# Three weight loads, each sent as a transfer of 120 partitions and a transfer of eight

## Chip, cores and metric

One Trainium2 chip, one of its cores. The metric is the device time of one execution in microseconds (us), lower is better. The kernel before was run three times: median 1458.31 us, 1456.86 to 1459.31. The profiler also recorded one execution, and all durations below come from that one.

## What is computed

The reference is a stack of transformer-like blocks on 256 tokens of width 1024, all in float32. The change lies in the expert layer of the first block:

```python
def one(xc):                                   # a chunk of 128 tokens
    q = (xc @ w_q).reshape(C, 8, 2, 128)       # 8 heads of queries, w_q is 1024 x 2048
    s = einsum('chpd,hpnd->chpn', q, subkeys)  # scores against 128 keys, twice a head
    sv, si = lax.top_k(s, 16)
    ...                                        # the 16 best of the 16 x 16 pairs: ids, g
    ue = jnp.take(u, ids, axis=0)              # rows of 1024 from a table of 16384
    ve = jnp.take(v, ids, axis=0)
    a = gelu(einsum('cd,chkd->chk', xc, ue))
    return einsum('chk,chkd->cd', g * a, ve)
```

Before it stands a mixer of differential and grouped-query attention, behind it stand two layers with a Fourier mixer, windowed attention and a gated feed-forward part.

## The kernel before, in words

The expert layer runs as 16 stages: 8 heads times 2 chunks of 128 tokens, with head h in stages 2h and 2h + 1. A stage has 16 gathers. One gather (L819, issued by GpSimd's queue) fetches, for each of the 128 tokens, one row of 2048 floats (the rows of `u` and `v` side by side, 8192 bytes), so it fills 128 partitions with 8192 bytes each: 1 MB. There are 256 gathers in all. They go into 13 places, some in the weight ring (`ring`), some in the scratch area (`arena`). A place is reused when the matmuls that read it are done (`pair_free`). For each gather VectorE makes the dot product with the token (L2273), ScalarE the GELU and a diagonal matrix of the weights (L1745, L1749), and TensorE adds the weighted rows with two matmuls (L1223).

Between the stages TensorE makes the queries of the next head (L1196) from that head's slice of `w_q`: 128 partitions by 8192 bytes, 1 MB. The slice of head 0 lies in the tile `wqb`, those of heads 1 to 4 are loaded ahead into tiles of their own. The slices of heads 5, 6 and 7 go into `wqb` too, one after the other, while the gathers run: these are the three loads of the change. SyncE's queue (SP) issues each (L783) once the matmuls that read the slice before it are done (`q_done`), and TensorE waits for it (L1192) before it makes the queries of that head. The semaphore `wq_in` counts 16 for each transfer.

Behind the third load SP waits for the last gather but one (L785) and for free ring places (L787), and then loads the weights of the first layer that follows (L789, L790, L752). SP has nothing else to issue during the gathers.

Of the kernel before, what the change touches and what calls it, by code (L numbers as in the profile page):

```python
# [21 lines left out]
KD = D // P  # L22
# [33 lines left out]
def in_end(b):  # L56

    return sum(IN_PIECES[:b + 1])
# [16 lines left out]
def slot_end(j):  # L75

    return max(p for p, (i, q) in enumerate(PIECE_AT) if i <= j) + 1
# [11 lines left out]
KEPT = 4  # L89
# [27 lines left out]
def place(n, k):  # L117
    return ORDER[TOPK * n + k]


def turn_of(n, k):
    return TURN[TOPK * n + k]
# [34 lines left out]
UNIT_HEADS = ((0, 4, 1, 5, 2, 6, 3, 7), (4, 5, 6, 7, 0, 1, 2, 3))  # L157
OUT_ORDER = (4, 5, 6, 7, 0, 1, 2, 3)
QPAIRS = ((0, 1), (2, 3), (4, 5), (6,), (7,))

class Chain:

# [19 lines left out]
def program(nc, x, ctx, const, lpar, b1w, wq, sk, uv, lw, out):  # L182
    with ExitStack() as stack:
# [3 lines left out]
        def sem(name):  # L187
            return stack.enter_context(nc.semaphore(name))
# [47 lines left out]
        def small(*shape):  # L236
# [126 lines left out]
        const_in, const2_in, x_in, ctx_in, lpar_in, sk_in, wq_in = (sem(n) for n in (  # L363
            "const_in", "const2_in", "x_in", "ctx_in", "lpar_in", "sk_in", "wq_in"))
# [57 lines left out]
        def lslot(j):  # L422
            return ring[:, (B1_SLOTS + j) % RING, :]
# [14 lines left out]
        def transposes(pe, g0, tiles, off=0, base=0):  # L438

            for i, blocks in enumerate(tiles):  # L440
                g = g0 + i
                tile_free(pe, g, off)
                for j, b in enumerate(blocks):
                    last = nc.tensor.transpose(ps[:, base + g % TB, j * P:(j + 1) * P], b, ident)
                last.then_inc(tile_done, 1)
# [100 lines left out]
        def ops_qk():  # L546
            return ([[(kT[:, k, :], 0, 512, None, None)] for k in range(5)]
                    + [[(qT[:, k, :], i * S, i * S + S, None, None) for i, k in enumerate(pair)] for pair in QPAIRS])

# [176 lines left out]
        @block.sync  # L726
        def _(sp):
            head = CO["lam"][0]
            sp.dma_start(cst[:, 0:head], const[:, 0:head]).then_inc(const_in, 16)
            def b1_used(n):  # L730

                if n < MOD_A:
                    sp.wait_ge(a_raw, n + 1)
                    sp.wait_ge(a_lo, 2 * (n + 1))
                elif n in IN_SLOT:
                    sp.wait_ge(in_lo, in_end(IN_SLOT.index(n)))
                else:
                    sp.wait_ge(mod_sum, KD * (MODB_SLOT.index(n) + 1))

            def l_used(l, j):  # L740

                if j == 3:
                    sp.wait_ge(yt_done, l * 2 + 2)
                elif j == 4:
                    sp.wait_ge(l_yf, l * 2 + 2)
                else:
                    sp.wait_ge(w_lo, l * PL + slot_end(j))

            def load_layer(l, j):
                n = B1_SLOTS + j  # L750
                w = SLOT_WIDTH.get(j, SLOT)
                sp.dma_start(ring[:, n % RING, 0:w], lw[l, j, :, 0:w]).then_inc(slot_in[n % RING], 16)  # L752


            for n in range(B1_SLOTS):
                if n >= RING:
                    b1_used(n - RING)
                w = 2048 if n == IN_SLOT[1] else SLOT
                at = SLOT // 2 if n < MOD_A else 0
                if at:  # L760
                    sp.dma_start(ring[:, n, 0:at], b1w[n, :, 0:at]).then_inc(half_in[n], 16)
                sp.dma_start(ring[:, n % RING, at:w], b1w[n, :, at:w]).then_inc(slot_in[n % RING], 16)
                if n == 1:
                    sp.dma_start(ctxr, ctx.rearrange("(c p) d -> p c d", p=P)).then_inc(ctx_in, 16)
                    sp.dma_start(xr[:, :, :], x.rearrange("(c p) d -> p c d", p=P)).then_inc(x_in, 16)
                if n == MOD_A + 1:
                    sp.dma_start(cst[:, head:CW], const[:, head:CW]).then_inc(const2_in, 16)
                    sp.dma_start(g1b, const[:, CW:CW + D]).then_inc(g1_in, 16)
            sp.dma_start(lps[:, :, :], lpar.rearrange("l p n -> p l n")).then_inc(lpar_in, 16)
            sp.wait_ge(modcol_done, MOD_A + MOD_B)  # L770
            sp.dma_start(wqb[:, :, :], wq[0, :, :].rearrange("p (k n) -> p k n", k=KD)).then_inc(wq_in, 16)
            sp.wait_ge(in_used, IP)
            sp.dma_start(skb[:, :], sk).then_inc(sk_in, 16)
            last = KEPT - 1
            sp.dma_start(wq_kept[:, :, :], wq[KEPT, :, :].rearrange("p (k n) -> p k n", k=KD)).then_inc(kept_in[last], 16)
            sp.wait_ge(sc_done, 16)
            for i in range(last):
                if i == 2:
                    sp.wait_ge(pt_done, 16)
                sp.dma_start(kept_wq[i], wq[i + 1, :, :].rearrange("p (k n) -> p k n", k=KD)).then_inc(kept_in[i], 16)  # L780
            for h in range(KEPT + 1, PH):
                sp.wait_ge(q_done, 1 if h == KEPT + 1 else h)
                sp.dma_start(wqb[:, :, :], wq[h, :, :].rearrange("p (k n) -> p k n", k=KD)).then_inc(wq_in, 16)  # L783

            sp.wait_ge(pair_in[place(STAGES - 1, TOPK - 2)], 16 * turn_of(STAGES - 1, TOPK - 2))  # L785
            for j in range(RING):
                sp.wait_ge(pair_free, NS + max(LAST_USE[2 * j], LAST_USE[2 * j + 1]))  # L787
                if j == 0:
                    sp.dma_start(lslot(0)[:, 0:2 * PIECE], lw[0, 0, :, 0:2 * PIECE]).then_inc(first_in, 16)  # L789
                    sp.dma_start(lslot(0)[:, 2 * PIECE:SLOT], lw[0, 0, :, 2 * PIECE:SLOT])\  # L790
                        .then_inc(slot_in[B1_SLOTS % RING], 16)
                else:
                    load_layer(0, j)
            for l in range(LAYERS):
                for j in range(RING, LSLOTS):
                    l_used(l, j - RING)
                    load_layer(l, j)
                for j in range(RING if l + 1 < LAYERS else 0):
                    l_used(l, LSLOTS - RING + j)
                    load_layer(l + 1, j)  # L800
            for i in range(4):
                c, part = i % 2, slice((i // 2) * 512, (i // 2 + 1) * 512)
                sp.wait_ge(dn_out, 4 * LAYERS - 3 + i)
                sp.dma_start(out[c * P:(c + 1) * P, part], xr[:, c, part]).then_inc(out_done, 16)
            sp.wait_ge(out_done, 64)
# [50 lines left out]
        def _(pe):  # L856
# [112 lines left out]
            for p, (b, q) in enumerate(IN_AT):  # L969
# [11 lines left out]
                if b == 4 and q == 1:  # L981
# [6 lines left out]
            transposes(pe, T_QK, [[krow[:, j, k * P:(k + 1) * P] for j in range(4)] for k in range(5)]  # L988
                       + [[qrow[:, j, k * P:(k + 1) * P] for k in pair for j in range(NC)] for pair in QPAIRS], base=TURN_BANK)
            pe.wait_ge(tile_act, T_BASE // 2)  # L990
# [196 lines left out]
            def all_queries(h):  # L1187

                if h <= KEPT:
                    pe.wait_ge(kept_in[h - 1], 16)  # L1190
                else:
                    pe.wait_ge(wq_in, 16 * (h - KEPT + 1))  # L1192
                head = kept_wq[h - 1] if h <= KEPT else wqb
                for s in range(2):
                    for k in range(KD):
                        last = nc.tensor.matmul(ps[:, 0, s * S:(s + 1) * S], head[:, k, s * P:(s + 1) * P], hT[:, k, :],  # L1196
                                                start=(k == 0), stop=(k == KD - 1))
                last.then_inc(q_done, 1)
# [14 lines left out]
            def keys(h):  # L1213

                all_queries(h)
                all_key_sums(h)
# [13 lines left out]
            back_to_rows(1, (0, 2))  # L1230
            pe.wait_ge(row_out, 4)
            all_queries(1)
            experts(0, 0, places=range(GROUP, 2 * GROUP))
            all_key_sums(1)
# [32 lines left out]
            for l in range(LAYERS):  # L1267
# [244 lines left out]
                for ft in range(FT):  # L1512
                    for t in range(2):
                        if ft >= 2:
                            pe.wait_ge(up_sum, l * 2 * FT + 2 * (ft - 2) + t + 1)
                        p = P_UP + 2 * ft + t
# [1192 lines left out]
```

## Time and profile before

| | |
|---|---|
| median of three runs | 1458.31 us |
| the profiled execution: its own time, its span | 1457.39 us, 1455.2 us |
| mean granted clock of TensorE | 0.965 |
| TensorE, VectorE, ScalarE, GpSimd busy | 90%, 76%, 44%, 21% |
| HBM read | 414.20 MB |
| gathers, all 256 | 36864 packets, 268.45 MB |
| transfers issued by SP | 13488 packets, 146.82 MB |

The span is the time from the first to the last instruction, and 2.2 us of the execution lie outside of it. Shares of busy time are means over stages with different limits: what a change in one stage is worth is read in that stage. "DMA share" is the mean busy share of the core's 16 DMA engines; it can stand a little over 1 because a packet's record overlaps the next one's.

### The profile page before, as it was taken

The numbers are of one execution on the slowest core, as the hardware profiler recorded it, in microseconds if no ns is written. First come the engines' busy times: TensorE is split into PE (matmuls) and PEld (weight loads), VectorE is DVE, ScalarE is ACT, GpSimd is POOL, SyncE is SP. The second block draws the span as 40 slices with busy tenths as digits, with TensorE's granted clock in tenths as the row PEclk, the third lists the DMA queues.
The fourth block names the chain that finished last, engine by engine and source line by source line (L and its number), as shares of the span: only waits on it lengthen the run. The fifth ranks groups of instructions, "written<-read, shape, count | busy, mean of one in ns | idle before, by whom it ended". The sixth has DMA issues, their size and how long they took to land.

```text
span 1455.2 us, 16512 instructions
## 1 busy us (share of the span) xinstructions
PE 1312.6 (90%) x5504; PEld 875.3 (60%) x5504; DVE 1109.0 (76%) x2316; ACT 633.1 (44%) x1322; POOL 310.5 (21%) x308
## 2 busy tenths in 40 slices
PE   9998898898797979698797799999999999999998
PEld 3876655453343424253343346678888887888887
DVE  6688857866776777766677777879998588799974
ACT  5343743312221222222222226567776455677752
POOL 0000004344444334344444430001111000011100
PEclk9999999999898989899898899999999999999999
DMA  9624468999999999999999997434544444345530
GB/s 391 275 116 184 164 255 330 420 421 422 408 421 422 421 421 421 422 421 421 419 416 408 419 422 281 166 125 147 201 175 176 154 140 169 116 180 194 206 145 29
DMA packets 50436, 416.31 MB, mean 286 GB/s; under 512 B 5552, under 2 KB 5680, under 8 KB 7088
## 3 DMA queue, kind: packets, MB, share of 16 engines
q0 software_dynamic: 36864, 268.45, 44.6%
q1 hardware_dynamic: 13488, 146.82, 26.4%
q8 instruction: 43, 0.70, 0.2%
q14 instruction: 41, 0.34, 0.1%
HBM read 414.20 MB, written 1.05 MB: 285 GB/s over the span
## 4 chain that ended last, share of the span: by engine, by line
PE 55%; DVE 20%; DMA 15%; issue 5%; ACT 3%; POOL 2%; DVEq 0%; SPq 0%; POOLq 0%; ACTq 0%
PE ps L1523 11%; PE ps L1223 9%; DMA ring<-in_uv,ids 8%; PE ps L1525 6%; DMA arena<-in_uv,ids 5%; PE ps L1313 4%; PE ps L1302 4%; PE ps L1310 4%; DVE ring L2273 3%; PE ps L1045 2%; DVE arena L2273 2%; PE ps L934 2%; PE ps L935 2%; PE ps L936 2%; PE ps L1196 1%
## 5 line engine op out<-in xcount | busy, mean ns | idle before, releaser
L1223 PE MATMUL ps<-ring,arena 128*128 128x512 f32 x632 | 293.9, 615 | 52.7 <-ACT arena L1749 52.6
L2273 DVE CUSTOM_DVE_ANT_0 ring<-ring,arena 128x1024 f32<-128x1024 f32 x158 | 190.4, 1224 | 86.3 <-DMA ring<-in_uv,ids 85.8
L1223 PEld LDWEIGHTS ps<-ring,arena 128*128 128x128 f32 x632 | 122.5, 197 | 214.4 <-issue 150.5
L1523 PE MATMUL ps<-hpair,arena_r 128*128 128x512 f32 x704 | 246.7, 395 | 0.0
L1223 PE MATMUL ps<-arena 128*128 128x512 f32 x392 | 188.7, 626 | 50.2 <-ACT arena L1749 50.2
L617 DVE TENSOR_TENSOR arena_r<-ring,arena_r 128x1024 fp32r<-128x1024 f32 x152 | 185.5, 1223 | 57.0 <-ACT arena_r L602 53.5
L819 POOL DMA_INDIRECT ring<-in_uv,ids x158 | 166.8, 1056 | 227.0 <-PE ps L1223 165.9
L1525 PE MATMUL ps<-hpair,arena_r 128*128 128x256 f32 x704 | 197.4, 280 | 0.0
L602 ACT ACTIVATE arena_r<-ring 128x1024 fp32r<-128x1024 f32 x152 | 159.1, 1054 | 58.0 <-PE ps L1313 53.9
L819 POOL DMA_INDIRECT arena<-in_uv,ids x98 | 106.7, 1089 | 358.6 <-issue 242.9
L1223 PEld LDWEIGHTS ps<-arena 128*128 128x128 f32 x392 | 77.1, 200 | 153.2 <-issue 91.9
L2273 DVE CUSTOM_DVE_ANT_0 arena<-arena 128x1024 f32<-128x1024 f32 x98 | 118.6, 1224 | 50.9 <-DMA arena<-in_uv,ids 50.6
L1523 PEld LDWEIGHTS ps<-hpair,arena_r 128*128 128x128 f32 x704 | 132.0, 187 | 30.9
L1749 ACT ACTIVATE arena<-cst,wts 128x128 f32<-128x128 f32 x256 | 87.9, 393 | 135.2 <-DVE wts L2266 82.6
L851 POOL TENSOR_TENSOR arena<-arena 128x256 f32<-128x256 f32 x44 | 36.1, 821 | 500.8 <-ACT arena L1891 500.8
L1525 PEld LDWEIGHTS ps<-hpair,arena_r 128*128 128x128 f32 x704 | 133.0, 189 | 0.0
L1745 ACT ACTIVATE gel<-dots 128x4 f32<-128x4 f32 (+2 forms) x68 | 13.9, 205 | 229.0 <-DVE dots L2273 229.0
L1302 PE MATMUL ps<-arena_r 128*128 128x512 f32 x240 | 67.3, 394 | 1.0 <-DVE arena_r L672 1.0
L1910 ACT ACTIVATE arena<-arena,lps 128x256 f32<-128x256 f32 x88 | 52.9, 602 | 32.7 <-DVE arena L2548 32.2
L1313 PE MATMUL ps<-arena_r 128*128 128x512 f32 x240 | 66.2, 390 | 0.0
L1310 PE MATMUL ps<-arena_r 128*128 128x512 f32 x240 | 66.2, 389 | 0.0
L2556 DVE SCALAR_TENSOR_TENSOR arena<-arena,lps 128x255 f32<-128x255 f32 x88 | 62.3, 708 | 0.0
(337 smaller groups left out, 1993.7 us busy)
## 6 DMA issues: line engine op xcount, KB each, us to landing
ring<-in_lw SPq DMA_DIRECT2D x39, 2048.0 KB, 7.8
ring<-in_b1w SPq DMA_DIRECT2D x14, 2048.0 KB, 8.8
ring<-in_b1w SPq DMA_DIRECT2D x9, 1024.0 KB, 16.8
ring<-in_lw SPq DMA_DIRECT2D x8, 1024.0 KB, 5.2
wqb<-in_wq SPq DMA_DIRECT2D x4, 1024.0 KB, 9.0
arena<-in_wq SPq DMA_DIRECT2D x3, 1024.0 KB, 13.4
ring<-in_uv,ids POOLq DMA_INDIRECT x158, 16.5
ring<-in_lw SPq DMA_DIRECT2D x2, 1088.0 KB, 9.9
```

The source lines that it names most:

```text
L602: nc.scalar.activation(high_of(l, p), piece_raw(p), ACT.Copy).then_inc(w_hi, 1)
L617: nc.vector.tensor_tensor(low_of(l, p), piece_raw(p), high_of(l, p).bitcast(F32), ALU.subtract)\
L819: pool.indirect_dma_start(pairs_at[at], None, uv, bass.IndirectOffsetOnAxis(ap=ids[:, c, k:k + 1], axis=0))\
L1223: last = nc.tensor.matmul(ps[:, 4 + 2 * c + b, :], diag[:, k % 4, :], vrows[place(n, k)][:, b * 512:(b + 1) * 512], start=(n == c and k == 0),
L1302: nc.tensor.matmul(dst, ah, high_of(l, p)[:, cols_], start=first, stop=False, skip_group_check=True)
L1310: last = nc.tensor.matmul(dst, al, high_of(l, p)[:, cols_], start=False, stop=end and rows_last, skip_group_check=True)
L1313: last = nc.tensor.matmul(dst, ah, low_of(l, p)[:, cols_], start=False, stop=end and not rows_last, skip_group_check=True)
L1523: nc.tensor.matmul(ps[:, bank, :].rearrange("p (t n) -> p t n", t=2), high_of(l, p)[:, cols_], hpair[:, :, k, :], start=(k == 0), stop=Fal ...
L1525: last = nc.tensor.matmul(ps[:, bank, S:2 * S], low_of(l, p)[:, cols_], hH[:, k, :], start=False, stop=(k == KD - 1), skip_group_check=True)
L1749: nc.scalar.activation(diag[:, k % 4, :], ident, ACT.Copy, scale=wts[:, c, k:k + 1])\
L2273: V.tensor_tensor_reduce(out=urows[at], in0=urows[at], in1=hrow[:, c, :], scale=1.0, scalar=0.0, op0=ALU.mult, op1=ALU.add, accum_out=dots ...
L2556: run(V.scalar_tensor_tensor(cx[:, 1:S], hx[:, 0:S - 1], cv[:, ft, 4 * t:4 * t + 1], cx[:, 1:S], ALU.mult, ALU.add))
```

## The change

Each of the three loads of `wqb` is issued as two transfers, first partitions 0 to 119, then partitions 120 to 127. The count that TensorE waits for is raised to match. The bytes, their source and their destination stay the same.

```diff
+WQ_ROWS = (slice(0, 120), slice(120, 128))
...
             for h in range(KEPT + 1, PH):
                 sp.wait_ge(q_done, 1 if h == KEPT + 1 else h)
-                sp.dma_start(wqb[:, :, :], wq[h, :, :].rearrange("p (k n) -> p k n", k=KD)).then_inc(wq_in, 16)
+                for rows in WQ_ROWS:
+                    sp.dma_start(wqb[rows, :, :], wq[h, rows, :].rearrange("p (k n) -> p k n", k=KD)).then_inc(wq_in, 16)
...
                 if h <= KEPT:
                     pe.wait_ge(kept_in[h - 1], 16)
                 else:
-                    pe.wait_ge(wq_in, 16 * (h - KEPT + 1))
+                    pe.wait_ge(wq_in, 16 + 16 * len(WQ_ROWS) * (h - KEPT))
```

## Rows read from the trace of the kernel before

**Rows 1.** The page, part 2: the span in 40 slices, the DMA lines.
```profile
DMA  9624468999999999999999997434544444345530
GB/s 391 275 116 184 164 255 330 420 421 422 408 421 422 421 421 421 422 421 421 419 416 408 419 422 281 166 125 147 201 175 176 154 140 169 116 180 194 206 145 29
```

**Rows 2.** Busy time by stretch, the whole of the saturated gathers.
```profile
core 0: us, PE busy (x) PEld busy (x) DVE busy (x) ACT busy (x) POOL busy (x), PEclk, DMA share, GB/s
243.00:850.00 607.00, 501.18 (x1257) 239.01 (x1256) 434.12 (x1085) 144.75 (x371) 258.94 (x242) 0.92 1.01 419
```

**Rows 3.** Waits of VectorE, 243 to 850 us: total us, times, longest.
```profile
DVE ring L2273 <- DMA ring<-in_uv,ids: 81.9, 66, 3.4
DVE arena L2273 <- DMA arena<-in_uv,ids: 47.5, 43, 1.3
```

**Rows 4.** The chain that ended last, 840 to 900 us: start, us, what.
```profile
857.58 20.47 DMA ring<-in_uv,ids
878.07 5.02 DMA ring<-in_lw
883.09 0.02 issue
883.11 1.06 ACT arena_r L602
884.17 0.02 issue
884.20 1.23 DVE arena_r L617
```

**Rows 5.** Busy time by stretch at the end of the gathers (columns as in rows 2).
```profile
870.00:873.00 3.00, 3.00 (x9) 1.32 (x8) 2.77 (x9) 0.20 (x1) 0.00 (x0) 1.00 1.03 423
...
874.00:875.00 1.00, 1.00 (x3) 0.38 (x2) 0.62 (x3) 0.28 (x2) 0.00 (x0) 1.00 0.55 229
875.00:876.00 1.00, 1.00 (x4) 0.51 (x3) 0.37 (x1) 0.33 (x1) 0.00 (x0) 1.00 0.16 66
...
877.00:878.00 1.00, 1.00 (x3) 0.38 (x2) 0.22 (x1) 0.50 (x2) 0.00 (x0) 1.00 0.06 25
```

**Rows 6.** DMA view, 876.25 to 878.75 us, in 40 slices.
```profile
GB/s 0 131 0 0 0 0 131 0 0 0 0 131 0 0 0 0 131 0 0 0 0 131 0 0 0 0 131 0 0 0 0 131 0 0 0 0 131 0 0 0
DMA packets 9, 0.07 MB, mean 26 GB/s; under 512 B 1, under 2 KB 1, under 8 KB 1
```

**Rows 7.** VectorE's last dot products, in order of time.
```profile
875.63 1.23 DVE L2273 CUSTOM_DVE_ANT_0 ring<-ring,arena 128x1024 f32<-128x1024 f32 x1 [0.74 <-DMA ring<-in_uv,ids]
...
878.07 1.23 DVE L2273 CUSTOM_DVE_ANT_0 ring<-ring,arena 128x1024 f32<-128x1024 f32 x1 [0.72 <-DMA ring<-in_uv,ids]
...
880.54 1.23 DVE L2273 CUSTOM_DVE_ANT_0 arena<-arena 128x1024 f32<-128x1024 f32 x1 [0.75 <-DMA arena<-in_uv,ids]
```

**Rows 8.** DMA view, 240 to 870 us: queues (packets, MB, share), issues.
```profile
q0 software_dynamic: 35791, 260.64, 99.8%
q1 hardware_dynamic: 432, 3.15, 1.2%
q8 instruction: 10, 0.16, 0.1%
q14 instruction: 18, 0.15, 0.1%
...
wqb<-in_wq SPq DMA_DIRECT2D x3, 1024.0 KB, 9.1
```

**Rows 9.** SP's second and third load of `wqb`, in order of time.
```profile
569.35 0.33 SPq L783 DMA_DIRECT2D wqb<-in_wq  x1
...
652.06 0.33 SPq L783 DMA_DIRECT2D wqb<-in_wq  x1
```

**Rows 10.** TensorE's use of the second and third load.
```profile
644.96 7.07 PE L1196 MATMUL ps<-hT,wqb 128*128 128x256 f32 x32
...
728.82 7.07 PE L1196 MATMUL ps<-hT,wqb 128*128 128x256 f32 x32
```

## The prediction

> **What bounds the kernel now.** I read the page's lines of slices first. The DMA engines are near full only in one stretch, slices 7 to 23, at about 421 GB/s [rows 1]; elsewhere TensorE carries the time. The stretch 243 to 850 us in one row shows a DMA share of 1.01, and TensorE 501, VectorE 434 and GpSimd 259 us busy of 607 [rows 2]. So the gathers are bound by DMA, not by an engine. VectorE's waits say the same: 81.9 + 47.5 = 129.4 us for gathers to land [rows 3]. 421 GB/s over 16 engines is 26.3 GB/s each, so a packet of 8192 bytes takes 0.311 us and eight of them 2.49 us. The 268.45 MB of 256 gathers are 128 rows of 8192 bytes each, eight rows to an engine if they are spread evenly.
>
> Then the end of the stretch, since a DMA-bound stretch is worth what it moves its last landing. The chain goes gather (landed 878.07), first layer weights (883.09), ScalarE, VectorE [rows 4]; the load at 878.07 stands behind SP's wait for the last gather but one. The reader should now look at the DMA share there: 1.03 to 873, 0.55 in 874 to 875, 0.16 in the next us and 0.06 in 877 to 878 [rows 5]. One engine of 16 is 0.0625. In 876.25 to 878.75 nine packets move, one each 0.31 us, at 26 GB/s [rows 6]: one engine is still at it alone, at full speed, with eight rows and one small packet, a whole gather's share. VectorE gets the last gathers at 875.63, 878.07 and 880.54, 2.45 us apart [rows 7], which is that engine's pace for eight rows. A gather is landed when its slowest engine is done, so **one engine sets every landing at the end**. The fifteen others were done with the last gather by about 876.2 (the share falls from 0.16 to 0.06 there, [rows 5]), the lagging one at 880.5 [rows 7]: a lag of 4.3 us. All sixteen were busy until 873, so what the last engine carries beyond the mean is paid in full.
>
> Why does it lag? Two queues of instruction fetches run beside the data: ten packets of 0.16 MB and eighteen of 0.15 MB in 240 to 870 us [rows 8]. At 26.3 GB/s they are 6.1 and 5.7 us of one engine. If the first queue is fixed to one engine and the second is spread, that engine would lag by 6.1 us less what the others get of the second: the size of the 4.3 us seen. This is my inference; no row names the engine of a packet.
>
> **The change, part by part.** A load of `wqb` is 128 rows of 8192 bytes: eight rows for each of 16 engines, 3 x 1 MB in all, 3.15 MB [rows 8].
>
> *The first part, 120 rows.* 120 is 15 x 8. Filled in eights, it leaves one engine without a row. That engine saves 8 x 0.311 = 2.49 us in each load, 7.5 us over three. The others keep their eight rows.
>
> *The second part, eight rows.* It goes to eight engines with one row each: +0.31 us on each of them a load, 0.93 us over three. The bytes stay the same; the sum over all engines is 0.
>
> *What lies on the path.* Only the last landing counts. If the engine left out is the lagging one, it would finish 7.5 us of work earlier, but the gain is capped by the next: the others' end, 4.3 us earlier. If the slowest of those is one of the eight with extra rows, it ends 0.93 us later than now, which leaves 3.4. Eight of sixteen have the rows and the share falls off over about 2 us [rows 5], so several engines are near each other and I take a value between, nearer the low end: 3.6 us. Bounds 3.0 and 4.3. The gain then goes through whole: VectorE waits 0.72 to 0.75 us for each of the last gathers [rows 7], the weights are issued when the last but one lands [rows 4], and with the share below 1 there is room for them. TensorE has 501 of 607 us of work in the stretch [rows 2], so it can follow.
>
> *The issues.* Each load costs SP one more instruction of 0.33 us [rows 9], 1 us in all. SP's queue has nothing else to issue until the gathers end; hidden. Without that cover it would be 1 us.
>
> *The wait of TensorE.* The load issued at 569.35 lands 9.1 us later [rows 8, 9] and is used at 644.96, the one of 652.06 at 728.82 [rows 10]: margins of 66 us. A second transfer behind the first adds at most its own row and a landing, far less. The count that TensorE waits for is that of both transfers; no engine waits longer. Cost 0; it would cost only if a load took over 66 us more.
>
> The Trainium skill ("DMA: Bandwidth & Descriptors", section "Why a DMA increments its semaphore by 16 and not by 1") says that a transfer runs on the largest number of engines up to 16 that divides its rows, taken from the lowest-numbered ones: 15 for 120 rows, which leaves out the last engine, and 8 for eight. The same page ("Latency and other measured facts") says that engines 7 and 15 are usually slower than the others in traces. Were the lagging engine 15, the sum would be the gain above; were it 7, a loss of 0.93 us. One engine does lag here, by 4.3 us, but no row gives its number.
>
> A rule of that page ("Rules for kernel authors") speaks against the change: splitting a transfer by partitions is not worth it, since the parts share the same engines. By it the sum would be 0. It tells nothing of a part that leaves an engine out.
>
> **The rivals.**
>
> *Forecast: the engine left out is the lagging one.* Speaks for it: exactly one engine lags [rows 5, 6], and an extra queue would be put at one end of the row of engines rather than in the middle, while rows dealt out in order leave the last one free. That is a judgement, not a row. 1457.4 - 3.6 = 1453.8 in the profiled execution. Chance 0.46.
>
> *Rival 1: the lagging engine is among the eight that take an extra row.* It then ends 3 x 0.31 = 0.93 us later and the engine relieved was never late: 1458.3 profiled. For it: eight of sixteen places, and the other end of the row is one of them. Chance 0.27.
>
> *Rival 2: it is among the seven that neither lose nor gain, or the split leaves no engine out* (the rows are spread over all sixteen some other way, so the change does not do what it says). No difference: 1457.4. Against the first half: it would lie in the middle. Chance 0.20.
>
> *Rival 3, the slower side: rows written by another engine than in a gather collide.* In the gathers, engine and partitions go together all the time. With 15 or 8 engines the partitions fall to others, and two engines may write into one group of partitions at once. If each of the 3 x 8 rows costs the lagging engine another packet's time, that is 24 x 0.311 = 7.5 us: 1464.9. It decides (over 2.9 us) from 0.12 us a row. No row shows a collision, as every large transfer here has 128 rows; against it, the loads are 1.2% of the engines' time [rows 8], and any collision with an engine that leads costs nothing up to 4.3 us. Chance 0.07.
>
> **How the numbers follow.** The profiled execution took 1457.39 us, 0.9 below the median of the runs, 1458.31. So the forecast is 1458.3 - 3.6 = 1454.7; rival 1 gives 1459.2, rival 2 1458.3, rival 3 up to 1465.8. The runs before spread from 1456.9 to 1459.3, so about 1.2 us must be allowed either way. The likeliest case alone has 1452.8 to 1456.5. Range: below, the full 4.3 us and 1.2 of spread, 1452.8; above, rivals 1 and 2 with their median's spread, 1459.8; left out are most of rival 3 and tails. 0.2% is 2.9 us, about what a measurement of this kernel can tell from no change. The forecast lies only 0.7 us beyond it, so of its 0.46 I count 0.40 as faster and 0.06 as same. With rivals 1 and 2 the same has 0.06 + 0.27 + 0.20 = 0.53, and slower 0.07.
>
> **What the profile after would show.** Right: in the us by us DMA shares at the end of the gathers, the stretch at 0.06 is gone and the share falls from 1 to near 0 within some 2 us; VectorE's last gather starts near 877 instead of 880.54, no longer at steps of one lone engine; the first layer load is issued near 874.5 instead of 878.07. The `wqb` loads appear as six issues, of 960 and 64 KB. Rival 1: the lone engine works on until about 881.5. Rival 2: nothing moves. Rival 3: data packets near the loads with shares above 1.01 and GB/s below 415. The prediction is wrong if the lone engine is still there, or if it is gone and TensorE, not DMA, then sets when the last experts end.

## The result, and the profile after

The change makes the kernel slower: 1470.9 us median of six runs (1469.64 to 1474.37) against 1458.51 us for the kernel before in the same session, a ratio of 1.0091 with a 95% interval of 1.0079 to 1.0103. The profiled execution has a span of 1469.4 us, 14.2 more than before. The forecast was 1454.7 us. By the medians the loss is 12.4 us; the profiled execution before lies 1.1 us below its median and the one after 0.9 us above. Each ratio in this document compares fast runs alone, which leaves out one run of the kernel without loads, at 3379.5 us.

The DMA view of the kernel after, 240 to 884 us in 40 slices of 16.1 us, shows where it went:

```profile
GB/s 346 379 420 417 417 420 422 422 421 422 421 420 421 420 421 421 422 421 422 422 415 309 422 421 399 423 321 408 421 397 408 422 420 422 415 396 421 421 422 422
...
q0 software_dynamic: 35792, 260.64, 99.1%
q1 hardware_dynamic: 453, 3.15, 1.9%
...
wqb<-in_wq SPq DMA_DIRECT2D x3, 960.0 KB
...
wqb<-in_wq SPq DMA_DIRECT2D x3, 64.0 KB
```

The rate is 420 GB/s as before [rows 1], but for three holes: slices 1 and 2, slice 22, slice 27, each at or just behind a load. (Smaller dips, to 396 to 408, have their like before, at 398 to 413 in slices of 15.75 us.) The same 3.15 MB of SP's transfers (q1) take 1.9% of the engines' time in place of 1.2%, and the same 260.64 MB of the gathers (q0) take 99.1% of 644 us in place of 99.8% of 630 us [rows 8]. For each engine that is about 12.2 against 7.6 us for the loads and 638.2 against 628.7 us for the gathers: 4.7 and 9.5 us more, 14.2 in all, which is the whole delay. Two thirds of it are gathers that became slower, one third the loads' own rows. Closer, busy time by stretch (PE, PEld, DVE, ACT, POOL busy, PEclk, DMA share, GB/s) of the first load, the same nine us in the kernel before and then after:

```profile
247.00:256.00 9.00, 8.26 (x30) 4.67 (x29) 7.21 (x27) 2.74 (x5) 3.67 (x4) 1.00 1.01 421
```

```profile
247.00:256.00 9.00, 8.26 (x27) 4.27 (x26) 6.98 (x31) 2.20 (x5) 4.89 (x5) 1.00 1.03 284
```

The DMA share stays at 1.03 while the rate is 284 GB/s. So the engines are not idle; their packets take longer. The same nine us after, in 40 slices, show that the first two are still at the old rate:

```profile
GB/s 400 473 401 473 364 437 437 473 364 328 218 255 109 291 291 255 255 291 255 255 218 218 291 218 291 255 146 255 291 255 218 146 255 255 255 255 146 255 182 328
```

The DMA view of 249 to 256 us, inside the load, gives the length of a packet:

```profile
q0 software_dynamic: 119, 0.87, 53.8%
q1 hardware_dynamic: 102, 0.84, 48.7%
```

0.84 MB are 102 packets of 8192 bytes. 48.7% of 16 engines times 7 us is 54.5 us, so one takes 0.53 us, not 0.31. The gathers beside them (0.87 MB, 106 data packets, 60.3 us) take 0.57 us each, not 0.31.

TensorE's queries of heads 5, 6 and 7, in the timeline of the kernel after:

```profile
566.90 7.07 PE L1199 MATMUL ps<-hT,wqb 128*128 128x256 f32 x32
...
654.64 7.07 PE L1199 MATMUL ps<-hT,wqb 128*128 128x256 f32 x32
...
743.08 7.07 PE L1199 MATMUL ps<-hT,wqb 128*128 128x256 f32 x32
```

The first of them in the kernel before:

```profile
562.25 7.07 PE L1196 MATMUL ps<-hT,wqb 128*128 128x256 f32 x32
```

The other two began at 644.96 and 728.82 [rows 10]: 4.7, 9.7 and 14.3 us of delay, one step of 4.6 to 5.0 us for each load. The lone engine at the end is still there; VectorE's last gathers and the shares at the end of the kernel after:

```profile
890.04 1.23 DVE L2276 CUSTOM_DVE_ANT_0 ring<-ring,arena 128x1024 f32<-128x1024 f32 x1 [0.74 <-DMA ring<-in_uv,ids]
...
892.45 1.23 DVE L2276 CUSTOM_DVE_ANT_0 ring<-ring,arena 128x1024 f32<-128x1024 f32 x1 [0.68 <-DMA ring<-in_uv,ids]
...
894.91 1.23 DVE L2276 CUSTOM_DVE_ANT_0 arena<-arena 128x1024 f32<-128x1024 f32 x1 [0.74 <-DMA arena<-in_uv,ids]
```

```profile
889.00:890.00 1.00, 1.00 (x4) 0.50 (x3) 0.22 (x1) 0.46 (x2) 0.00 (x0) 1.00 0.28 115
890.00:891.00 1.00, 1.00 (x4) 0.45 (x3) 0.95 (x1) 0.00 (x0) 0.00 (x0) 1.00 0.08 33
...
892.00:893.00 1.00, 1.00 (x4) 0.50 (x3) 0.55 (x1) 0.20 (x1) 0.00 (x0) 1.00 0.06 25
```

The same picture as [rows 5, 7], 14.4 us later (894.91 against 880.54).

### The profile page after: what moved, and what is told of

It is laid out like the page before. It is cut to its first block, busy times and chain, and to the rows that moved or that the text cites. A ratio compares the mean times of both kernels' runs of the same rounds, so it can differ in the third digit from the quotient of the medians.

```text
span 1469.4 us, 16515 instructions
## 1 busy us (share of the span) xinstructions
PE 1314.6 (89%) x5504; PEld 875.8 (60%) x5504; DVE 1108.9 (75%) x2316; ACT 632.2 (43%) x1322; POOL 311.2 (21%) x308
## 4 chain that ended last, share of the span: by engine, by line
PE 52%; DVE 21%; DMA 16%; issue 5%; ACT 2%; POOL 2%; DVEq 0%; SPq 0%; POOLq 0%; ACTq 0%
PE ps L1526 11%; DMA ring<-in_uv,ids 9%; PE ps L1226 7%; DMA arena<-in_uv,ids 6%; PE ps L1528 6%; PE ps L1305 4%; PE ps L1316 4%; PE ps L1313 4%; DVE ring L2276 4%; DVE arena L2276 2%; PE ps L1048 2%; PE ps L937 2%; PE ps L939 2%; PE ps L938 2%; POOL ring L822 1%
## 5 line engine op out<-in xcount | busy, mean ns | idle before, releaser
L822 POOL DMA_INDIRECT ring<-in_uv,ids x158 | 171.1, 1083 | 236.4 <-PE ps L1226 170.9
L822 POOL DMA_INDIRECT arena<-in_uv,ids x98 | 103.2, 1053 | 362.9 <-issue 242.4
```

The costliest lines, as they stand in the source:

```text
L822: pool.indirect_dma_start(pairs_at[at], None, uv, bass.IndirectOffsetOnAxis(ap=ids[:, c, k:k + 1], axis=0))\
```

## The experiments

The theory after the result is that of the third rival. As the experiments were planned it reads: a transfer of another number of partitions gives each engine other partitions than a gather does, and engines that write into one group of partitions wait for each other. Against it stand three others: counts that leave engines out or unevenly loaded, two transfers in place of one, and the order of the rows in HBM. Each ratio is against runs of the kernel before on the same chip. "Last gather" is the start of VectorE's last dot product of a gather (before: 880.54 us).

**112 and 16 partitions.**

```diff
-WQ_ROWS = (slice(0, 120), slice(120, 128))
+WQ_ROWS = (slice(0, 112), slice(112, 128))
```

> The three loads as 112 and 16 partitions. If the loss (12.4 us at the median, 4.8 us a load in the trace) comes from leaving an engine out or from an uneven count of rows (15 engines, then 8), it is gone here, since 112 and 16 are multiples of 16: within 2 us of the kernel before. If it comes from partitions falling to other engines than in the gathers, it stays, as seven rows an engine shift them too: plus 9 to 15 us, with packets of about 0.5 us near the loads. If two transfers in place of one cost it, it stays too, at 12 us.

Measured: 1.0076 (1.0058 to 1.0093), last gather 890.53 us, and 269 GB/s in 247 to 256 us. Most of the loss is there although both counts are multiples of 16, so uneven counts can't be the main cause. Whether they add anything is open, as the interval overlaps that of the change.

**Two transfers by columns.**

```diff
-                for rows in WQ_ROWS:
-                    sp.dma_start(wqb[rows, :, :], wq[h, rows, :]...
+                for ks in (slice(0, 4), slice(4, 8)):
+                    sp.dma_start(wqb[:, ks, :], wq[h, :, :].rearrange("p (k n) -> p k n", k=KD)[:, ks, :])...
```

> Each of the three loads as two transfers of all 128 partitions, each with half of the columns (4096 bytes a row). The row to engine assignment is that of one whole load. If the number of transfers costs the time, plus 12 us; if the partitions of a transfer do, no change from the kernel before (within 2 us), and a rate of about 420 GB/s while they run.

Measured: 0.9984 (0.9974 to 0.9993), last gather 880.36 us. Its stretch of the first load, columns as above (the rate before is 421):

```profile
247.00:256.00 9.00, 8.26 (x32) 5.05 (x31) 7.35 (x29) 3.59 (x6) 3.65 (x4) 1.00 1.02 422
```

Two transfers cost nothing when each has all 128 partitions.

**One load split.** Heads 6 and 7 are loaded whole.

```diff
-                for rows in WQ_ROWS:
+                for rows in (WQ_ROWS if h == KEPT + 1 else (slice(0, P),)):
...
-                    pe.wait_ge(wq_in, 16 + 16 * len(WQ_ROWS) * (h - KEPT))
+                    pe.wait_ge(wq_in, 32 + 16 * (h - KEPT))
```

> Only the load of head 5 is split in 120 and 8 partitions, those of heads 6 and 7 stay whole. If each split load slows the transfers beside it and nothing is given back or added later, a third of the loss: plus 4 to 5 us. If the loss grows from one load to the next (a backlog, or gathers shifted against TensorE), clearly less than a third.

Measured: 1.003 (1.0017 to 1.0043), last gather 885.44 us, 4.9 later. A third of the loss for a third of the loads; nothing is given back later.

**64 and 64 partitions.** `WQ_ROWS` is `(slice(0, 64), slice(64, 128))`.

> The three loads as two halves of 64 partitions, four rows for each of 16 engines. If only counts that are no multiple of 16 are slow, no change. If partitions on other engines than in the gathers are the cause: in fours, half of the engines keep their partitions and half do not, so a loss between zero and that of the change, plus 4 to 12 us. If two transfers are the cause, plus 12 us.

Measured: 1.0065 (1.0046 to 1.0084), last gather 893.19 us, 282 GB/s in 247 to 256 us. I had expected half of the engines to be spared. They are not, which fits if an engine that keeps its partitions is slowed too by the one that joins it there.

**The load of head 0 split, no gather beside it.**

```diff
-            sp.dma_start(wqb[:, :, :], wq[0, :, :].rearrange("p (k n) -> p k n", k=KD)).then_inc(wq_in, 16)
+            for rows in (slice(0, 120), slice(120, 128)):
+                sp.dma_start(wqb[rows, :, :], wq[0, rows, :].rearrange("p (k n) -> p k n", k=KD)).then_inc(wq_in, 16)
```

The three loads during the gathers are whole, and the counts are raised by 16.

> The load of head 0 (L771), issued before the gathers begin, is split in 120 and 8; the three loads during the gathers stay whole. Before, it lands 7.8 us after its issue, with two other 1 MB loads behind it and no gather beside it. If partitions on other engines than usual make the engines of one and the same transfer collide, its packets take about 0.5 us here too and the landing comes some 2 us later; if the collision needs the gathers beside it, packets stay at 0.31 us. Time: no change either way, as the load is used at 209 us, except if the loads behind it come so late that the gathers start later: at most plus 2 us.

Measured: 1.0002 (0.999 to 1.0013). The stretch 188 to 196 us, first of the kernel before, then of this one:

```profile
188.00:196.00 8.00, 8.00 (x39) 4.77 (x36) 3.58 (x8) 3.14 (x9) 0.00 (x0) 1.00 1.02 425
```

```profile
188.00:196.00 8.00, 8.00 (x39) 4.69 (x38) 4.09 (x9) 2.56 (x9) 0.00 (x0) 1.00 1.00 271
```

GpSimd has issued nothing yet; only SP's transfers run. The rate still falls. The DMA view of 192 to 198 us has 1.20 MB at 96.3% of the engines, 0.63 us a packet. So the engines of one transfer of 120 partitions collide with each other, or with SP's next transfers, and no gather is needed. Here it costs nothing, as nobody waits.

**Eight extra transfers of 8, every fourth partition.** Into `wq_kept`, which nothing reads any more, behind the load of head 7 of the kernel before. SP waits for them at its end.

```diff
+                for rows in ([slice(at + r, at + 29 + r, 4) for at in (0, 32) for r in range(4)] if h == PH - 1 else ()):
+                    sp.dma_start(wq_kept[rows, :, :], wq[h, rows, :]...).then_inc(kept_in[last], 16)
```

> The kernel before, with eight more transfers of 8 partitions right behind the load of head 7, into a tile that nothing reads any more (the same rows of weights, 0.5 MB, result unused). Each takes every fourth partition, so that with one row an engine and groups of four partitions dealt to the engines in turn, each engine writes a partition that is its own in a gather. If mismatched partitions are the cause, these packets stay at 0.31 us, the rate at 420 GB/s, and the cost is eight more rows on eight engines: plus 2.5 us if the lagging engine is one of the eight, nothing if it is not (the others have 4.3 us in hand).

Measured: 1.001 (0.9999 to 1.0021), last gather 883.30 us, 2.8 later. The interval just holds 1, so the cost rests on the last gather of one execution; the run with the destination of every fourth partition, below, repeats it.

**The same with 8 partitions next to each other.** The slices are `slice(8 * i, 8 * i + 8)` for `i` in 0 to 7.

> As the run with every fourth partition: the same 64 rows in eight transfers of 8 partitions behind the load of head 7, but now 8 partitions next to each other in each. If mismatched partitions are the cause, packets of 0.5 us and more, a rate well under 400 GB/s while they run, and plus 5 to 10 us; if only small transfers or the use of eight engines cost, the same as its sister run.

Measured: 1.0055 (1.0035 to 1.0076), last gather 889.86 us, 9.3 later. The stretch 655 to 670 us, first with every fourth partition, then with neighbours:

```profile
655.00:670.00 15.00, 13.50 (x31) 5.92 (x32) 7.06 (x15) 2.90 (x10) 6.89 (x7) 1.00 1.02 423
```

```profile
655.00:670.00 15.00, 12.59 (x25) 5.42 (x26) 4.53 (x9) 2.44 (x9) 5.61 (x5) 0.89 1.03 299
```

Same bytes, same number of transfers, same count of partitions: 423 against 299 GB/s. Only which partitions go together differs. Inside the extra transfers, in 661 to 673 us, the DMA view of the run with neighbours is:

```profile
q0 software_dynamic: 298, 2.17, 88.1%
q1 hardware_dynamic: 113, 0.46, 13.9%
```

The gathers' packets take 0.64 us there (265 data packets, 169.2 us). And 2.63 MB in 12 us are 219 GB/s. If the transfers of eight used eight engines and the other eight ran on at 26.3 GB/s each, those would move 2.52 MB of it, and 0.11 MB would be left, less than the 0.46 MB of the extra rows themselves. And a share of 102% leaves next to no engine idle. So on that dealing engines that carry none of the extra rows are slowed too. How is not shown.

**The 120 part alone.** The changed kernel with `WQ_ROWS = (slice(0, 120),)`; the last eight partitions of heads 5 to 7 keep other weights.

> The changed kernel without the transfers of eight partitions: partitions 120 to 127 of heads 5, 6 and 7 keep the weights of head 0 (part of the load is left out). If the 120 part carries the loss, plus 10 to 12 us against the kernel before and about 1 to 3 us less than the change; if the transfer of eight does, no loss or a gain.

Measured: 1.0082 (1.0064 to 1.01), last gather 891.08 us, 10.5 later. The 120 part carries most of the loss. What the transfers of eight add is not settled: the last gathers of the two profiled executions differ by 14.4 - 10.5 = 3.9 us, but the medians lose 12.4 and 11.4 us, and the intervals of the ratios overlap.

**Destination or source.** The extra transfers again, with the two sides taken apart: written to neighbours and read from every fourth row, and the reverse.

```diff
+                fourth = [slice(at + r, at + 29 + r, 4) for at in (0, 32) for r in range(4)]
+                beside = [slice(8 * i, 8 * i + 8) for i in range(8)]
+                for to, rows in (zip(beside, fourth) if h == PH - 1 else ()):
+                    sp.dma_start(wq_kept[to, :, :], wq[h, rows, :]...).then_inc(kept_in[last], 16)
```

> Eight extra transfers of 8 behind the load of head 7, as before with the result unused, written to 8 partitions next to each other but read from every fourth row of the weights. If the destination's partitions cause the collision: like the run with both contiguous, plus 6 to 9 us. If the order of rows in HBM does: like the one with every fourth partition, plus 1 to 3 us.

Measured: 1.0055 (1.0037 to 1.0073), last gather 890.57 us, 10.0 later.

> The reverse: written to every fourth partition, read from 8 rows of the weights next to each other. If the destination causes it: plus 1 to 3 us, packets of 0.31 us; if the order in HBM does: plus 6 to 9 us.

Measured for the reverse: 1.0015 (1.0002 to 1.0027), last gather 883.01 us, 2.5 later. The same stretch of both, first the destination of neighbours, then that of every fourth:

```profile
655.00:670.00 15.00, 12.09 (x28) 5.29 (x29) 4.98 (x11) 2.76 (x9) 5.88 (x6) 1.00 1.04 301
```

```profile
655.00:670.00 15.00, 14.17 (x32) 5.92 (x32) 6.98 (x13) 2.51 (x9) 7.59 (x7) 1.00 1.01 422
```

The destination's partitions decide, 301 against 422 GB/s; the order in HBM does not.

**No loads at all.** The loop of the three loads is left out of the kernel before, and heads 5 to 7 use head 0's weights.

> The kernel before without the three loads: the queries of heads 5 to 7 are made with head 0's weights. Every engine has 24 rows less. If the engine that lags sets the end through its number of rows, the end of the gathers comes 24 times 0.311 = 7.5 us sooner and so does the end of the kernel: minus 7 to 8 us, with the lone engine's stretch as long as before. If something else sets the end, clearly less.

Measured: 0.9967 (0.9944 to 0.9989), a median 6.9 us lower; last gather 876.08 us, 4.5 earlier. The shares at the end:

```profile
871.00:872.00 1.00, 1.00 (x4) 0.52 (x3) 0.84 (x1) 0.00 (x0) 0.00 (x0) 1.00 0.14 57
872.00:873.00 1.00, 1.00 (x3) 0.39 (x3) 0.61 (x3) 0.28 (x2) 0.00 (x0) 1.00 0.06 25
873.00:874.00 1.00, 1.00 (x4) 0.41 (x3) 0.38 (x1) 0.32 (x1) 0.00 (x0) 1.00 0.06 25
```

The lone engine stays. In this execution GpSimd issued the first gather at 224.96 us, against 223.12 before (the others lie within 0.8 us of that), so from first gather to last it took 651.1 and not 657.4 us: 6.3 us less for 24 rows an engine, of the 7.5 expected. The interval of the ratio, 1.6 to 8.2 us, does not settle whether the missing 1.2 us are real.

**Columns once more.**

> The kernel with two transfers by columns once more, in five rounds: its ratio was 0.9984 with an interval that just left out 1. No theory here gives a gain: the bytes of each engine are the same. If it was chance, the interval holds 1; if halves of rows do help, 0.998 again.

Measured: 0.999 (0.998 to 1.0001). Whether the split by columns gains a tenth of a per cent stays open; by this interval the gain is not over 0.2%. No other version that computes the whole result beats the kernel before.

## Why the prediction was wrong

**What bounds the kernel** was read rightly: the delay of every load arrives whole at the end, 4.7, 9.7 and 14.3 us at the three queries, 14.4 at the last gather, 14.2 in the span (12.4 by the medians).

**The step that failed** is the one that priced a row moved to another engine as the row alone: "The others keep their eight rows", eight at 0.311 us, and "+0.31 us on each of them a load". It took for granted that an engine's time goes with its number of rows only. The runs show in its place that the rows of a load split by partitions take 0.53 us each, and the gathers' rows beside them 0.57 us. Over the three loads that is 4.7 us more on each engine for the loads' rows and 9.5 us for the gathers' rows: 1.6 and 3.2 us a load, where the prediction had a saving for one engine and at most 0.31 us for the others. The run with the 120 part alone has 10.5 / 3 = 3.5 us a load. What the part of eight adds, put at 0.31 us, is not settled.

**Rival 3** named this mechanism, at a chance of 0.07, with 7.5 us for 24 rows. Of its mechanism the paired runs show the outer part: the destination's partitions decide, everything else equal. That two engines meet in one group of partitions is inferred, and since engines without an extra row are slowed too it is not the whole. Its price was wrong in both terms: it charged 0.31 us more on each of a load's rows, where about 0.2 was measured, and nothing on the gathers' rows beside them, which are two thirds of the loss. Its argument against itself, that a collision with an engine in the lead costs nothing up to 4.3 us, failed too: the lagging engine is slowed like the others.

**Which engine is relieved.** The forecast needed the lagging engine to be the one left out. The lone engine of the end is unchanged after the change, so it hardly was. The extra transfers on every fourth partition use eight engines with eight rows each by the reckoning put down with the run, and delay the last gather by 2.8 and 2.5 us, near 8 x 0.311 = 2.5. In the three runs that should leave it alone (both by columns, and the early split) it starts at 880.36 to 881.08 us, so executions differ by less than that. An engine in the lead would not have shown. So the lagging engine is most likely among the eight that a transfer of eight rows uses: the identity was that of rival 1. That alone would have cost 0.93 us and stayed inside the range. What leaving out the lagging engine would gain was therefore not tried; the run without loads only shows that 24 rows less on every engine are worth most of their 7.5 us.

**Engines and partitions.** The Trainium skill's rule for transfers of fewer partitions ("DMA: Bandwidth & Descriptors", "Why a DMA increments its semaphore by 16 and not by 1") agrees with the place of the lagging engine as far as the runs show it: eight rows reach it. The Trainium skill's note on the slow engines 7 and 15 (same page, "Latency and other measured facts") would then mean 7, and no row gives the number. The Trainium skill's rule against splitting by partitions (same page, "Rules for kernel authors") expected no gain, and there was a loss of 0.9%. A further page of the Trainium skill, "SBUF — State Buffer", section "Door 1: The DMA port swizzle", has 16 ports of eight partitions each, in groups of four (0 to 3 with 32 to 35, and so on). By it eight neighbours reach two ports and eight taken by fours reach eight. The trace agrees with 299 against 423 GB/s. That rows of a transfer other than a whole one of 128 are dealt out in neighbouring runs is inferred from this; no run names an engine.

**The hidden terms** held: SP's extra issues and the landings are not waited for by TensorE, whose queries start without a wait for a load in the kernel after.

## What to carry to other kernels

Before splitting a transfer by partitions, ask which partitions each part writes. Here a split by partitions slowed its own packets and those of the gathers beside it, and the gathers' share of the loss was the larger; a split by columns that keeps all 128 partitions cost nothing. Price what a transfer does to its neighbours, and not its own rows alone. Read the DMA share together with the GB/s: a share of 1.03 at 284 GB/s is not more work done, but longer packets. An engine that lags can be helped only by taking work off that very engine, and the trace has to say which it is before the gain is counted.

## What the hardware showed that I had not expected

While the parts of a load split by partitions run beside the gathers, the rate is 243 GB/s (120 and 8, 249 to 256 us), 261 (112 and 16, 248 to 255) and 226 (64 and 64, 250 to 257) in place of 419, although bytes and rows of 8192 bytes are the same. It falls without any gather beside it too, to 271 against 425 GB/s. And two halves of 64 partitions lose nearly as much (12.7 us at the last gather) as 120 and 8 (14.4 us).
